# Forget-gate and stick-breaking heads walked in pairs, their value products alternating, and value products issued ahead of the transposes

## The chip, the cores and the metric

One NeuronCore of one Trainium2 chip runs the whole program. The metric is device time in microseconds (us) of one execution. A chip run of this kernel takes 1867.9 us in the median of three (1865.4 to 1868.3).

## The reference, cut to what matters

Two transformer blocks run one after the other on 512 tokens of width 1024, in fp32. The change lies in the first block, which has two layers. In a layer, after one input projection, three kinds of attention heads work side by side:

```python
# differential heads (4, value width 128): two score maps, softmax of each, w = p1 - lam * p2, then w @ v
# forget-gate heads (4, width 64):
logits = s + cqb[..., :, None] - cum_logf[..., None, :]
p = jax.nn.softmax(jnp.where(causal, logits, -jnp.inf), axis=-1)
return jnp.einsum('bhqk,bhkd->bhqd', p.astype(v.dtype), v)
# stick-breaking heads (4, width 64):
log_fail = jnp.where(strict, jax.nn.log_sigmoid(-z), 0.0)
after = lax.cumsum(log_fail, axis=3, reverse=True) - log_fail
weights = jnp.where(strict, jnp.exp(jax.nn.log_sigmoid(z) + after), 0.0)
return jnp.einsum('bhqk,bhkd->bhqd', weights.astype(v.dtype), v)
```

The head outputs are gated with silu of a projection, joined, projected with `w_out`, added to the residual and normalised. The second block has latent-attention and sparse-attention heads of width 128, a gated recurrence and a feed-forward part.

## The kernel before

**Steps.** A planner in plain Python (`plan`, L199) writes one list of steps, and each engine walks that list and issues its own share of every step. So the list is the order of work on each engine's queue, and semaphores tie the queues together.

**Items.** Attention is cut into items: one head, one tile of 128 queries, and all keys up to that tile, so tiles 0 to 3 have 1 to 4 blocks of 128 keys. Kinds are A (differential), B (forget-gate), C (stick-breaking), M (latent) and X (sparse). In a layer of the first block 16 items of kind A come first (items 0 to 15 in layer 0), then 16 of B (16 to 31) and 16 of C (32 to 47). The B and C items are laid out at L449 to L458. A unit is what shares one output bank: for A, M and X one head, for B and C two heads, of which the even one (`e=0`) writes partitions 0 to 63 of the bank and the odd one partitions 64 to 127. Before, the unit's items run e=0 tile 0 to 3, then e=1 tile 0 to 3.

**Stages and ticks.** `stages` (L240) gives each stage of an item and its lag. `tick` (L253) moves the pipeline by one item n and writes, in this order: the scores of item n, its first softmax part, the second part of n-1, the third of n-2 (kind C alone), the transposes of n-3, and the value products of n-4. What each does:

- scores (L1629, mask at L1633): TensorE, into one of two score banks. A score product must wait until the softmax of the item two before has read its bank: for kind B its logits (`soft1_done`), for kind C `soft2_done` (L1616 to L1623).
- soft1: for A, M, B and X a VectorE maximum (B: logits at L2191, maximum at L2195) and a ScalarE exponential (L1838 for B). For C three ScalarE activations, a log of one plus an exponential (L1708 to L1710).
- soft2: for B one VectorE product (L2213). For C VectorE's sum, scan and difference (L2229, L2232, L2235). soft3, C alone: ScalarE's exponential (L1855).
- trans: TensorE turns the probabilities, one transpose for each key block, into the single bank T (L1658), after the copy of the item before has emptied it. ScalarE copies T out (L1863) into one of two places PT, once the value products of the item two before are through with that place.
- pv: TensorE's value products, one for each key block (L1672), V as the stationary operand: 64 columns of it for B and C, 128 for A, M and X. They wait for that copy (L1663).

Each fp32 product shows as two matmul records in the trace.

**What lies between ticks.** `weave` (L298) places projections between ticks. A projection of 128 output columns has 24 matmuls; while items of kinds B and C are walked it is cut into two halves of 12, with a tick between and one after. For items 25 to 40 these are the gate projections. When one is whole, ScalarE and VectorE take the gate through L1708 to L1710, L2083, L1819, L2133 and L2143; in their queues that stands before the softmax of the next, even-numbered item. Weights are split by ScalarE (L1973) and GpSimd (L1435) into a high and a low part. After the last gate come splits of the gated outputs (L1989, L2456), three part projections of 18 matmuls (L1502) between ticks 40 and 44, and then `flush` (L286), which issues the remaining ticks, 44 to 51, with nothing between. The second block places its M and X ticks by hand with `paced` (L329).

## Time and profile before

| What | us |
|---|---|
| median of three runs | 1867.9 |
| the profiled execution, whole | 1866.4 |
| its span in the profile | 1864.6 |
| TensorE matmuls busy | 1730.1 (93%) |
| TensorE weight loads busy (beside the matmuls) | 1311.8 (70%) |
| VectorE busy | 864.3 (46%) |
| ScalarE busy | 799.2 (43%) |
| GpSimd busy | 594.1 (32%) |
| 16 DMA engines | 79 GB/s over the span |

The profile is one execution. Busy time is the time in which an engine had at least one instruction under way; matmuls overlap one another, so the spacing of their starts says more than their length. "PEclk" is the clock granted to TensorE as a share of the full 2.4 GHz. The mean over the span was 0.956. The first layer's items of kinds B and C run from 205 to 381 us, the second layer's from 591 to 767 us.

### The profile page before, as it was taken

The page shows a single profiled execution, that of the slowest core. Times are in us where ns is not written, and L with a number is a line of the kernel's source. Part 1 is how long each engine was busy: PE and PEld are TensorE (multiplying, and loading weights), DVE is VectorE, ACT ScalarE, POOL GpSimd, SP SyncE. Part 2 cuts the span into 40 slices and gives each one's busy share as a digit, 9 for nine tenths or more (in the row PEclk, how much of TensorE's full clock was granted, in tenths as well). Part 3 has the DMA queues.
Part 4 walks back from the last instruction along what each step waited for, and adds up shares of the span by engine and source line. Part 5 has one row for each costly group of instructions (what it writes and reads, how often), then busy time and mean ns, then how long its engine had stood idle before and what let it go on. Part 6 is the DMA issues. An engine that isn't in the chain of part 4 may idle for free. (4 is left out here: it accounts for less than half of the span.)

```text
span 1864.6 us, 21015 instructions
## 1 busy us (share of the span) xinstructions
PE 1730.1 (93%) x7750; PEld 1311.8 (70%) x7750; DVE 864.3 (46%) x1487; ACT 799.2 (43%) x1512; POOL 594.1 (32%) x291
## 2 busy tenths in 40 slices
PE   7999999889999998989998999998999899999997
PEld 4766766578667665677564777777787788888786
DVE  5543335553533345454598548475556222221402
ACT  3334446533344455344323555565643334443411
POOL 2613212135313121144120332333265424444440
PEclk9998999899989998999999999999999989999999
DMA  6412222014222120114121222322274333333221
GB/s 177 108 34 68 57 57 68 12 61 112 57 57 57 53 83 23 46 46 130 34 65 51 73 80 68 125 74 68 89 240 135 90 89 93 102 91 102 90 79 45
DMA packets 203832, 148.81 MB, mean 80 GB/s; under 512 B 14926, under 2 KB 183506, under 8 KB 203732
## 3 DMA queue, kind: packets, MB, share of 16 engines
q1 hardware_dynamic: 199056, 132.45, 24.9%
q0 software_dynamic: 4528, 14.95, 2.4%
q8 instruction: 63, 1.03, 0.2%
q14 instruction: 37, 0.30, 0.1%
q10 hardware_dynamic: 148, 0.07, 0.0%
HBM read 136.96 MB, written 10.49 MB: 79 GB/s over the span
## 5 line engine op out<-in xcount | busy, mean ns | idle before, releaser
L1435 POOL TENSOR_TENSOR weights_rounded<-weights_raw,weights_rounded 128x1024 fp32r<-128x1024 f32 (+1 forms) x237 | 566.7, 2406 | 1146.8 <-ACT weights_rounded L1973 1146.7
L1506 PE MATMUL proj<-hT_high,weights_rounded 128*128 128x512 f32 (+1 forms) x1904 | 640.2, 408 | 17.5 <-POOL weights_rounded L1435 7.5
L1506 PEld LDWEIGHTS proj<-hT_high,weights_rounded 128*128 128x128 f32 x1904 | 369.7, 195 | 108.4 <-issue 23.7
L1506 PE MATMUL proj<-hT_low,weights_rounded 128*128 128x512 f32 (+1 forms) x952 | 378.9, 398 | 0.0
L1973 ACT ACTIVATE weights_rounded<-weights_raw 128x1024 fp32r<-128x1024 f32 (+1 forms) x237 | 234.0, 1008 | 112.4 <-DMA weights_raw<-in_w_ffn_down 59.0
L1502 PE MATMUL proj<-weights_rounded,hT_high 128*128 128x512 f32 (+1 forms) x640 | 203.9, 395 | 22.2 <-DVE branches_low L2456 13.5
L1506 PEld LDWEIGHTS proj<-hT_low,weights_rounded 128*128 128x128 f32 x952 | 186.0, 195 | 38.8 <-issue 3.7
L1502 PEld LDWEIGHTS proj<-weights_rounded,hT_high 128*128 128x128 f32 x640 | 122.3, 195 | 50.9 <-issue 15.7
L1629 PE MATMUL score<-qk 64*128 64x256 f32 (+3 forms) x256 | 81.0, 501 | 18.6 <-ACT E L1835 10.2
L1672 PE MATMUL attn_out<-probs_T,V 128*64 128x128 f32 (+1 forms) x560 | 89.2, 294 | 0.0
L1658 PE MATMUL turned_probs<-constants,probs 128*128 128x128 f32 x320 | 61.8, 295 | 18.5 <-ACT probs_T L1863 18.2
L1672 PEld LDWEIGHTS attn_out<-probs_T,V 128*64 128x64 f32 (+1 forms) x560 | 68.8, 169 | 11.7 <-issue 10.0
L2175 DVE TENSOR_REDUCE small<-score 128x1 f32<-128x128 f32 (+3 forms) x64 | 28.3, 483 | 99.1 <-PE score L1633 99.1
L1502 PE MATMUL proj<-weights_rounded,hT_low 128*128 128x512 f32 (+1 forms) x192 | 72.5, 378 | 0.0
L1629 PEld LDWEIGHTS score<-qk 64*128 64x128 f32 x256 | 29.7, 190 | 54.9 <-issue 41.9
L1506 PE MATMUL score<-hT_high,weights_rounded 128*128 128x512 f32 (+2 forms) x208 | 65.4, 392 | 0.0
L1835 ACT ACTIVATE E<-score,small 128x128 f32<-128x128 f32 (+3 forms) x64 | 33.2, 524 | 68.4 <-DVE small L2175 68.4
L1708 ACT ACTIVATE tg<-proj 128x512 f32<-128x512 f32 x31 | 18.5, 597 | 101.7 <-PE proj L1506 101.7
L1754 ACT ACTIVATE qk<-proj 128x512 f32<-128x512 f32 x30 | 17.9, 597 | 92.0 <-PE proj L1506 92.0
L1863 ACT ACTIVATE probs_T<-turned_probs 128x128 f32<-128x128 f32 (+3 forms) x128 | 54.1, 423 | 5.3 <-PE turned_probs L1658 5.3
L1658 PEld LDWEIGHTS turned_probs<-constants,probs 128*128 128x128 f32 x320 | 37.8, 150 | 25.9 <-DVE probs L2213 15.1
L2083 DVE SCALAR_TENSOR_TENSOR tg<-proj,tg 128x512 f32<-128x512 f32 x20 | 13.8, 692 | 90.5 <-ACT tg L1710 90.5
(473 smaller groups left out, 2779.8 us busy)
## 6 DMA issues: line engine op xcount, KB each, us to landing
weights_raw<-in_w_in SPq DMA_DIRECT2D x113, 512.0 KB, 4.0
weights_raw<-in_w_out SPq DMA_DIRECT2D x24, 512.0 KB, 3.8
weights_raw<-in_w_ffn_gate SPq DMA_DIRECT2D x22, 512.0 KB, 3.9
weights_raw<-in_w_ffn_up SPq DMA_DIRECT2D x22, 512.0 KB, 3.8
weights_raw<-in_w_ffn_down SPq DMA_DIRECT2D x22, 512.0 KB, 3.5
gates<-constants POOLq DMA_DIRECT2D x24, 256.0 KB, 3.0
weights_raw<-gates SPq DMA_DIRECT2D x24, 256.0 KB, 3.6
weights_raw<-in_w_in SPq DMA_DIRECT2D x20, 256.0 KB, 3.2
```

Of the source, the lines that this page charges most:

```text
L1435: nc.gpsimd.tensor_tensor(piece_view(WR, p, "raw"), piece_view(WF, p, "raw"), piece_view(WR, p, "high"), ALU.subtract).then_inc(w_low, 1)
L1502: mm = nc.tensor.matmul(ps[:, 0:gr["N"]], x_[:, k, t * P:(t + 1) * P], w_[:, 0:gr["N"]], start=first, stop=last)
L1506: mm = nc.tensor.matmul(ps[:, on], w_[:, c0:c0 + P], x_[:, k, on], start=first, stop=last)
L1629: nc.tensor.matmul(ps[:, 0:K], qk[r, it["q"], tq], qk[r, it["k"], 0:K], start=True, stop=False)
L1658: mm = nc.tensor.transpose(T[:, j * P:(j + 1) * P], PR[:, i % 3, j * P:(j + 1) * P], cn("ident"))
L1672: mm = nc.tensor.matmul(O[u % 2][r0:r0 + rn, t * P:(t + 1) * P], v, PT[:, i % 2, j * P:(j + 1) * P], start=(j == 0), stop=(j == t))
L1708: link(nc.scalar.activation(dst, src, ACT.Abs, **kw))
L1754: nc.scalar.activation(plain[dst[0]](dst[1]), ps[:, :], ACT.Copy, scale=gr["scale"])\
L1835: ins = nc.scalar.activation(e[:, j, :], sc[(first_map[n] + j) % SCORE_BANKS][:, 0:K], ACT.Exp, bias=nmax[:, c + j:c + j + 1], accum_out=s ...
L1863: nc.scalar.activation(PT[:, i % 2, 0:it["K"]], T[:, 0:it["K"]], ACT.Copy).then_inc(turned_out, 1)
L1973: nc.scalar.activation(piece_view(WR, p, "high"), piece_view(WF, p, "raw"), ACT.Copy).then_inc(w_high, 1)
L2175: ins = nc.vector.tensor_reduce(nmax[:, c + j:c + j + 1], sc[(first_map[n] + j) % SCORE_BANKS][:, 0:K], AX, ALU.max, negate=True)
```

## The change

Three things are changed. The items of a B or C unit run tile by tile, e=0 and e=1 of tile 0, then both of tile 1, and so on, so that a tick's number of key blocks goes 1,1,2,2,3,3,4,4. The value products of the two items of a pair are issued together, in the tick in which the odd one is due, block by block with the two heads alternating. And in every tick, of all kinds, the value products (of n-4) are issued before the transposes (of n-3).

```diff
-    stages = [("scores", 0), ("soft1", 0), ("soft2", 1), ("soft3", 2), ("trans", 3), ("pv", 4)]
+    stages = [("scores", 0), ("soft1", 0), ("soft2", 1), ("soft3", 2), ("pv", 4), ("trans", 3)]
...
+                if name == "pv" and it["kind"] in "BC":
+                    if it["rows"][0]:
+                        steps.append(("pv", (n - lag - 1, n - lag)))
+                    continue
+                if name == "pv":
+                    steps.append(("pv", (n - lag,)))
                     continue
...
-                for e in range(2):
-                    for t in range(NT):
+                for t in range(NT):
+                    for e in range(2):
...
-                    it = items[arg]
-                    u, t, i = it["unit"], it["tile"], turned_at[arg] - 1
-                    pe.wait_ge(turned_out, i + 1)
+                    its = [items[n] for n in arg]
+                    u, t = its[0]["unit"], its[0]["tile"]
+                    pe.wait_ge(turned_out, turned_at[arg[-1]])
...
                     for j in range(t + 1):
-                        v = avv[:, j, :] if it["kind"] == "X" else V[:, j, v0:v0 + vn]
-                        mm = nc.tensor.matmul(O[u % 2][r0:r0 + rn, t * P:(t + 1) * P], v,
-                                              PT[:, i % 2, j * P:(j + 1) * P], start=(j == 0), stop=(j == t))
-                    mm.then_inc(pv_done, 1)
+                        for it, n in zip(its, arg):
+                            i = turned_at[n] - 1
+                            r0, rn = it["rows"]
+                            v0, vn = it["v"]
+                            v = avv[:, j, :] if it["kind"] == "X" else V[:, j, v0:v0 + vn]
+                            mm = nc.tensor.matmul(O[u % 2][r0:r0 + rn, t * P:(t + 1) * P], v,
+                                                  PT[:, i % 2, j * P:(j + 1) * P], start=(j == 0), stop=(j == t))
+                            if j == t:
+                                mm.then_inc(pv_done, 1)
```

No product, transpose, copy or transfer is added or taken away.

## Rows read from the trace of the kernel before

**Rows 1.** Busy us by window: length, PE, PEld, DVE, ACT, POOL, clock, DMA, GB/s.

```profile
224.00:300.00 76.00, 72.67 (x331) 49.16 (x331) 31.00 (x67) 35.55 (x76) 15.48 (x8) 0.98 0.24 70
300.00:345.00 45.00, 35.56 (x147) 24.35 (x146) 27.92 (x39) 28.93 (x59) 9.72 (x4) 0.91 0.11 36
345.00:385.00 40.00, 36.41 (x153) 23.96 (x153) 16.67 (x27) 19.41 (x43) 1.18 (x1) 0.81 0.00 0
```

**Rows 2.** TensorE's waits from 224 to 385: us in total, times, longest.

```profile
PE proj L1502 <- DVE branches_low L2456: 6.8, 3, 3.0
PE turned_probs L1658 <- ACT probs_T L1863: 5.3, 5, 1.5
PE score L1629 <- DVE logits L2235: 4.2, 3, 2.6
```

**Rows 3.** Timeline of TensorE, tick of item 23: start, length, instruction, count.

```profile
238.60 1.12 PE L1629 MATMUL score<-qk 64*128 64x512 f32 x2
...
239.72 0.28 PE L1658 MATMUL turned_probs<-constants,probs 128*128 128x128 f32 x1
239.94 1.09 PE L1672 MATMUL attn_out<-probs_T,V 128*64 128x128 f32 x8
240.95 0.50 PE L1506 MATMUL proj<-hT_high,weights_rounded 128*128 128x512 f32 x1
241.29 0.40 PE L1506 MATMUL proj<-hT_low,weights_rounded 128*128 128x512 f32 x1
```

**Rows 4.** Timeline of TensorE, a tick of a differential head.

```profile
116.86 0.70 PE L1629 MATMUL score<-qk 64*128 64x256 f32 x4
...
117.94 0.61 PE L1672 MATMUL attn_out<-probs_T,V 128*128 128x128 f32 x4
```

**Rows 5.** Timeline of TensorE, scores of items 44 and 45.

```profile
364.26 0.49 PE L1629 MATMUL score<-qk 64*128 64x128 f32 x2
...
365.43 0.70 PE L1629 MATMUL score<-qk 64*128 64x256 f32 x2
```

**Rows 6.** Timeline of TensorE, first score records of items 26 and 34 to 40.

```profile
252.66 0.59 PE L1629 MATMUL score<-qk 64*128 64x384 f32 x1
...
296.71 0.59 PE L1629 MATMUL score<-qk 64*128 64x384 f32 x1
...
302.42 1.12 PE L1629 MATMUL score<-qk 64*128 64x512 f32 x2 [0.46 <-DVE logits L2235]
...
307.72 0.37 PE L1629 MATMUL score<-qk 64*128 64x128 f32 x1
...
314.50 0.48 PE L1629 MATMUL score<-qk 64*128 64x256 f32 x1 [2.58 <-DVE logits L2235]
...
320.71 0.59 PE L1629 MATMUL score<-qk 64*128 64x384 f32 x1
...
327.14 0.69 PE L1629 MATMUL score<-qk 64*128 64x512 f32 x1 [1.18 <-DVE logits L2235]
...
332.44 0.37 PE L1629 MATMUL score<-qk 64*128 64x128 f32 x1
```

**Rows 7.** Timeline of TensorE, ticks 27 and 29; brackets: idle before, releaser.

```profile
260.07 0.30 PE L1658 MATMUL turned_probs<-constants,probs 128*128 128x128 f32 x1 [0.94 <-ACT probs_T L1863]
260.30 0.85 PEld L1672 LDWEIGHTS attn_out<-probs_T,V 128*64 128x64 f32 x8
...
270.76 0.52 PE L1658 MATMUL turned_probs<-constants,probs 128*128 128x128 f32 x3 [1.46 <-ACT probs_T L1863]
```

**Rows 8.** Timeline of VectorE, scans of stick-breaking items of 1 and 4 blocks.

```profile
366.35 0.42 DVE L2232 TENSOR_TENSOR_SCAN E<-E 128x128 f32<-128x128 f32 x1
...
374.30 1.22 DVE L2232 TENSOR_TENSOR_SCAN E<-E 128x512 f32<-128x512 f32 x1
```

**Rows 9.** Busy time after the wait at 270.76, columns as in rows 1.

```profile
271.00:275.00 4.00, 4.00 (x15) 2.98 (x14) 0.65 (x3) 1.42 (x4) 2.37 (x1) 0.59 0.03 8
```

**Rows 10.** Timeline of TensorE, value products of items 46 and 47.

```profile
378.45 2.95 PE L1672 MATMUL attn_out<-probs_T,V 128*64 128x128 f32 x14
```

More of the change, by code:

```diff
@@ L259, in tick @@
                 if (it["kind"] == "I" and lag >= 2) or (name == "soft3" and it["kind"] != "C"):
+                    continue
+                if name == "pv" and it["kind"] in "BC":
+                    if it["rows"][0]:
+                        steps.append(("pv", (n - lag - 1, n - lag)))
+                    continue
+                if name == "pv":
+                    steps.append(("pv", (n - lag,)))
                     continue
@@ L1660, in _ @@
                 elif op == "pv":
-                    it = items[arg]
-                    u, t, i = it["unit"], it["tile"], turned_at[arg] - 1
-                    pe.wait_ge(turned_out, i + 1)
+                    its = [items[n] for n in arg]
+                    u, t = its[0]["unit"], its[0]["tile"]
+                    pe.wait_ge(turned_out, turned_at[arg[-1]])
                     if u >= 2:
                         unit_done(pe, u - 2)
-                    for gg in it["values"]:
-                        wait_group(gg)
-                    r0, rn = it["rows"]
-                    v0, vn = it["v"]
+                    for it in its:
+                        for gg in it["values"]:
+                            wait_group(gg)
                     for j in range(t + 1):
-                        v = avv[:, j, :] if it["kind"] == "X" else V[:, j, v0:v0 + vn]
-                        mm = nc.tensor.matmul(O[u % 2][r0:r0 + rn, t * P:(t + 1) * P], v,
-                                              PT[:, i % 2, j * P:(j + 1) * P], start=(j == 0), stop=(j == t))
-                    mm.then_inc(pv_done, 1)
+                        for it, n in zip(its, arg):
[7 more added lines that the diff above has]
+                                mm.then_inc(pv_done, 1)
                 elif op == "down":
```

## The prediction

> **What bounds the kernel now.** I read the page's busy shares first: TensorE works 1730.1 us, 93% of the span, so time taken from it counts unless it was waiting anyway. The change touches both layers of the first block, whose two copies run alike, so I worked one out and doubled it. The busy times by stretch [rows 1] part that layer in three: forget-gate heads (72.7 of 76 us busy), then the stick-breaking heads beside the gate projections (35.6 of 45), then the last stick-breaking pair with little beside it (clock 0.81). The waits there [rows 2] say who is late: a rounded activation, ScalarE's copy of the turned probabilities, and VectorE's stick-breaking logits. The 32 items of a layer are numbered 16 to 47 below, four tiles a head, lengths of 1 to 4 key blocks ("units").
>
> **What a value product costs.** In the tick of item 23 [rows 3] eight records (four products, two records each) take 1.01 us from their start to the next projection, 0.109 each, 0.218 a unit. Around them the array changes shape. A transpose is 0.11 of stream, yet 0.22 passes before the first value record; the eight are 0.14 longer than their stream; the first projection record takes 0.34 and not 0.23. Together 0.36 us a visit to the half-width shape. A differential head, whose product is full width, shows none of that [rows 4].
>
> **Part 1, alternating halves.** The even head writes partitions 0 to 63 of the output bank, the odd one 64 to 127. No place of the trace switches between column halves. The nearest rows are the differential scores, on two halves of the array's rows: four records of 64x256 take 0.70 us, as the two of one head do [rows 4, 5]. So two halves can stream at once, here for split rows and not split columns. Bounds: a pair's unit costs from 0.218 (both at once) to 0.436 (one after the other). I take 0.218, being nearest to those rows. Its four weight loads a unit, 0.106 apart for eight in 0.85 [rows 7] when paced by the matmuls, leave an open point. The Trainium skill ("TensorE: Matmul & The Clock Gate", Packing small matmuls) reports column packing as about as good as row packing, but says in the same section that weight loads overlap running matmuls only when the row group differs. By the Trainium skill's second sentence the halves, which share all rows, would expose their loads; the trace shows loads hidden within one half [rows 7], and nothing of a switch. Rival 4 is that case.
>
> The naive sum: 80 pair units in two layers at 0.218 saved is 17.4 us, 32 fewer visits at 0.36 is 11.5 us, 28.9 us off TensorE. I don't expect it, for what follows.
>
> **Part 2, value products only in odd ticks, and tile lengths 1,1,2,2,3,3,4,4.** I went through the layer from one score product to another.
> - Items 16 to 25, until 252.66; TensorE waits for no one here. A score costs 0.21 more a unit [rows 5]. Before, score lengths sum to 10 (16-19) and 13 (20-25), after 6 and 16: -0.2 net. Value products of ticks 20-25: 13 units at 0.218 and six visits become 6 pair units at 0.218 and three visits, -2.6. Sum -2.8.
> - Items 26 to 39, start 252.66 to 332.44 [rows 6]. A gate projection ends before each even item, and then ScalarE and VectorE work through the gate (log, minimum, exponential, products) before they serve the item. For forget-gate items the next odd tick waits for the copy of the last head's turned probabilities, 7.4 us after item 26's score with 3 units in the item and 4 in the copy (252.66 to 260.07, of it idle 0.94), less with 1 and 2 units (idle 1.46) [rows 6, 7]. The value product that used to fill part of this wait moves to the odd tick. So its removal from the even tick is worth nothing. The chain stays: 7.0, 6.95 and 7.65 us with the new lengths, while TensorE is through after 4.85, 4.85 and 5.4: waits near 2.0, 1.9 and 2.0 in place of 0.94, 1.46, 0.92. Added up with the odd ticks (pair, transposes, 2.9 for the half projection), 252.66 to 296.71 becomes 42.1 against 44.05, of which 1.55 was low clock (next paragraph): -0.4 without it. For stick-breaking items the odd score waits for VectorE's logits of two items before. These cost 1.0, 1.6, 2.1 and 2.7 us at 1 to 4 units (scan 0.42 to 1.22, two others 0.29 to 0.69) [rows 8]. The waited-for lengths become 1, 2, 3 and were 2, 4, 2, so 5.2, 5.7 and 7.0 us from the even score in place of 5.7, 6.8 and 6.4. 296.71 to 332.44 becomes 31.95 against 35.73 with 1.5 of low clock: -2.25. Waits: 1.1, 1.8, 2.8.
> - The clock. After the wait of 1.46 the granted clock is 0.59 over 271 to 275, the 1.2 GHz level for most of it, which takes 1.64 us of TensorE's time, say 1.55 net; after 0.94 nothing falls [rows 7, 9]. The waits of 1.46 and 2.58 were both followed by it, two spells a layer. Now five waits are at 1.8 to 2.8; I estimate four of them with a spell, 2.2 more at 1.55: +3.4 (from -3.1, none left, to +4.7).
> - 332.44 to 345.7: ScalarE and VectorE work off gate and splits, TensorE waits up to 3.0 us for them [rows 2]; unchanged, 0.
> - 345.74 to 364.26, ticks 41 to 43. Scores 9 to 5 units, partly at the low clock, -1.3; transposes +0.3; pairs -1.2; a wait for item 38's copy, now issued later, +0.3. Sum -1.9.
> - The end, 364.26 to 381.40, where nothing lies beside it [rows 10]. Before, items 44 to 47 have 1,2,3,4 units, now 3,3,4,4. By durations in proportion to those of [rows 8] the last score goes from 6.0 to 7.4 us after the start and its probabilities are ready 14.6 and not 12.65 in. Then copy 45, pair (44,45), transposes 46, copy, transposes 47, copy and pair (46,47) follow strictly, since the pair now stands ahead of the transposes. Ends 18.5 at full clock, 21.0 at half, before 17.1. As before it runs at the half rate from 374 on, and now idles more: +2.9, between +1.4 and +3.9.
>
> **Part 3, value products ahead of transposes in single-head items.** Both wait for the same copy, so no wait is added. The turned copy is issued up to 0.87 later; a group of 24 matmuls, some 5.5 us, lies between ticks and hides it. ScalarE's queue stands behind it meanwhile, but it idles there. Only in the emptying of the sparse heads (1338 to 1344) nothing is between: +0.8, bounds 0 to +1.5. No DMA and no queue of SP or POOL is moved: the splits stand where they stood.
>
> **The sum.** A layer: -2.8 -0.4 -2.25 +3.4 -1.9 +2.9 = -1.05. Two: -2.1. With +0.8: -1.3 us on the profiled execution, whose own time is 1866.4 (span 1864.6): 1865.1. The median of the runs, 1867.9, is 1.5 above it, so I predict 1866.6.
>
> **Rivals.**
> 1. *The waits lengthen but the clock does not follow.* For: 0.94 and 1.18 us did no harm. Against: 1.46 did, and TensorE does less around them now. No more spells than two, and the end at +1.4: -2.8 -2.65 -1.9 +1.4 = -5.95 a layer, -11.1 with part 3: 1856.8.
> 2. *TensorE's saved time simply comes off*, as it would if the copies were early everywhere: -28.9, 1839. Against: the waits of [rows 2, 7].
> 3. *Slower: the two column halves don't stream at once.* Then nothing is saved by alternating, and products that filled waits are now exposed in odd ticks: 34 pair units a layer (6, 17, 7, 4 in the four stretches) at 0.218 is 7.4, and 0.9 more at the end's half clock; 16.6 for both: 1883. It decides from about a third of the overlap lost (5 us). For: no row shows split columns together. Against: the split rows. The same time comes out if the program alternates but the array keeps order.
> 4. *Weight loads stand exposed at each switch.* Four loads of 0.106 a pair unit, 34 units, twice: 29 more on top of rival 3, 1912. For: nothing in the rows. Against: within one half the loads are hidden [rows 7].
>
> **How the numbers follow.** Forecast 0.42 (1860 to 1873; 0.10 of it faster, 0.22 within, 0.10 slower), rival 1 0.26, rival 2 0.06, rival 3 0.22, rival 4 0.04. A measurement of this kernel tells about 0.2% (3.7 us) from no change. Faster 0.42, same 0.22, slower 0.36. The range reaches from below rival 1 to rival 3: 1852 to 1884, leaving out 0.06 and a little below it, and rival 4 with half the spread of rival 3 above, some 0.2 in all. The likeliest case's own range is 1860 to 1873.
>
> **What would show it.** Overlap: sixteen value records of a 4-unit pair in about 1.0 us, not 1.9. Waits: ScalarE's copy some 2 us late in three odd ticks a layer, now ahead of value products; five and not two stretches near 0.5 clock. The end of a layer at 18.5 to 21 us from item 44's score. I am wrong if gate chains shorten with TensorE's work, if spells of low clock stay at two, or if pair records come 0.109 apart.

## The result

The changed kernel takes 1872.15 us in the median of 20 runs (1867.8 to 1873.6), the kernel before 1866.9 in 20 runs beside them. The ratio is 1.0028, with a 95% interval of 1.0020 to 1.0035: slower by 0.28%, 5.2 us. I had forecast 1.3 us less than before. The range of 1852 to 1884 held the time, the sign was wrong. The profiled execution of the changed kernel took 1868.3 us (span 1866.5), so it is one of its shorter ones; its span is only 1.9 us above that of before. Six of the 20 runs took 1867.8 to 1869.4 us at a mean granted clock of 0.948 or 0.949, as this one did; the other fourteen took 1870.85 us or more, twelve of them at 0.946 or 0.947. So of the 5.2 us the traces can show about 2.

### The profile after

The head of the page, in the columns of the table of before:

```profile
span 1866.5 us, 20983 instructions
PE 1712.0 (92%) x7750; PEld 1300.9 (70%) x7750; DVE 866.6 (46%) x1487; ACT 799.6 (43%) x1512; POOL 596.2 (32%) x291
```

TensorE is busy 18.1 us less, yet the span is 1.9 us longer: all that was saved, and 2 us more, is now idle time. The three windows of [rows 1] again (length, busy time of PE, PEld, DVE, ACT, POOL, then granted clock, DMA share, GB/s):

```profile
224.00:300.00 76.00, 68.28 (x342) 47.28 (x341) 34.16 (x70) 38.57 (x84) 17.37 (x9) 0.96 0.20 63
300.00:345.00 45.00, 33.46 (x137) 22.26 (x136) 24.39 (x35) 26.34 (x52) 8.08 (x4) 0.86 0.11 36
345.00:385.00 40.00, 33.61 (x146) 21.78 (x145) 16.05 (x24) 17.73 (x38) 2.37 (x1) 0.68 0.00 0
```

Busy time fell by 4.4, 2.1 and 2.8 us, and the clock from 0.98, 0.91, 0.81 to 0.96, 0.86, 0.68. TensorE's waits in the same stretch (us in total, times, longest), against [rows 2]:

```profile
PE attn_out L1682 <- ACT probs_T L1874: 9.0, 7, 2.1
PE proj L1509 <- DVE branches_low L2467: 8.6, 3, 4.5
PE score L1636 <- DVE logits L2246: 6.3, 4, 2.7
PE turned_probs L1665 <- ACT probs_T L1874: 1.7, 2, 0.9
```

The copy of the turned probabilities is now waited for mostly by the value products and no longer by the transposes, 10.7 us in all where it was 5.3. The wait of 4.5 us ahead of the second part projection is 1.5 us longer than before, but the way from item 40's score to item 41's is not: 12.8 us against 13.3, with less of it at the low clock.

**The pair itself works as hoped.** A pair of three blocks, and two pairs of four, in TensorE's timeline (start, length, instruction, count, [idle before, releaser]):

```profile
242.84 0.88 PE L1682 MATMUL attn_out<-probs_T,V 128*64 128x128 f32 x12
...
253.96 1.76 PE L1682 MATMUL attn_out<-probs_T,V 128*64 128x128 f32 x16 [2.12 <-ACT probs_T L1874]
...
297.80 1.09 PE L1682 MATMUL attn_out<-probs_T,V 128*64 128x128 f32 x16
```

Sixteen records take 1.09 us, what eight took for one head. A pair of n blocks costs what a single head's n blocks cost (0.44, 0.66, 0.88, 1.09 us for 1 to 4). The second line has the forecast wait ahead of such a pair, and the pair is longer there, 1.76 us, as the clock falls within it (next paragraph).

**The clock.** Four short windows of the same layer, behind the waits at 253.96 (2.12 us), 266.57 (2.06), 307.56 (1.78) and 320.59 (2.72), and the two ends of the layers:

```profile
254.30:257.30 3.00, 3.00 (x19) 2.38 (x16) 0.12 (x1) 1.81 (x5) 2.37 (x1) 0.50 0.00 0
268.00:271.00 3.00, 3.00 (x9) 2.32 (x8) 0.00 (x0) 0.34 (x2) 1.92 (x1) 0.50 0.03 8
309.00:312.00 3.00, 3.00 (x10) 2.43 (x9) 0.55 (x1) 1.84 (x5) 2.13 (x1) 0.50 0.00 0
322.60:325.60 3.00, 3.00 (x10) 2.42 (x9) 2.07 (x2) 2.05 (x4) 0.30 (x1) 0.50 0.00 0
...
360.00:384.00 24.00, 18.73 (x73) 11.25 (x72) 11.16 (x15) 11.86 (x22) 2.37 (x1) 0.50 0.00 1
749.00:773.00 24.00, 18.75 (x71) 11.48 (x72) 10.46 (x14) 11.19 (x21) 2.38 (x1) 0.50 0.00 1
```

A clock of 0.50 is the 1.2 GHz level for the whole window. All four spells are short. The last two lines are the new thing: 24 us on end at half rate where the layer ends, in both layers (the clock record has 23.9 us, from 360.0 and from 749.2). Before, the spell there was 6.8 us long (from 374.1).

**The end of the layer.** From item 44's score to the output projection:

```profile
356.33 0.91 PE L1636 MATMUL score<-qk 64*128 64x384 f32 x2
...
359.64 0.44 PE L1682 MATMUL attn_out<-probs_T,V 128*64 128x128 f32 x4 [1.12 <-ACT probs_T L1874]
360.01 0.69 PE L1665 MATMUL turned_probs<-constants,probs 128*128 128x128 f32 x2
361.35 2.07 PE L1636 MATMUL score<-qk 64*128 64x512 f32 x2 [0.65 <-DVE logits L2246]
...
369.25 0.87 PE L1665 MATMUL turned_probs<-constants,probs 128*128 128x128 f32 x3 [0.90 <-ACT probs_T L1874]
370.70 1.55 PE L1682 MATMUL attn_out<-probs_T,V 128*64 128x128 f32 x12 [0.58 <-ACT probs_T L1874]
372.18 1.12 PE L1665 MATMUL turned_probs<-constants,probs 128*128 128x128 f32 x4
374.07 1.09 PE L1665 MATMUL turned_probs<-constants,probs 128*128 128x128 f32 x4 [0.78 <-ACT probs_T L1874]
375.85 1.97 PE L1682 MATMUL attn_out<-probs_T,V 128*64 128x128 f32 x16 [0.69 <-ACT probs_T L1874]
379.39 0.77 PE L1509 MATMUL proj<-weights_rounded,hT_high 128*128 128x512 f32 x1 [1.57 <-DVE branches_low L2467]
```

The drain, from item 44's score to the end of the last value product, is 21.5 us; before it was 17.1 [rows 5, 10]. The projection behind it starts at half rate: 0.77 us for its first record. Its first 114 matmuls take 28.2 us from 379.39, before 26.1.

Stretches from score to score in the two traces, in us, layer 0 | layer 1 (from the first score record of the item named; the end of the drain is that of the last value product):

| Stretch | before | after | difference | forecast |
|---|---|---|---|---|
| items 16 to 26 | 47.7, 47.7 | 45.0, 45.0 | -2.7, -2.7 | -2.8 |
| items 26 to 40 | 79.8, 79.7 | 80.2, 78.6 | +0.5, -1.1 | +0.75 (-0.4 -2.25 +3.4) |
| items 40 to 44 | 31.8, 31.8 | 29.1, 30.3 | -2.7, -1.5 | -1.9 |
| drain | 17.1, 17.1 | 21.5, 21.5 | +4.4, +4.4 | +2.9 |
| first 114 matmuls of the projection | 26.1, 26.1 | 28.2, 28.6 | +2.1, +2.5 | 0 |
| from there to the next layer or block | 58.2, 84.4 | 59.3, 82.7 | +1.1, -1.7 | 0 |

Part of these differences is the low clock's place. Over items 40 to 44 it covers 13.6 us before in both layers, and after 6.8 us in layer 0 and 13.6 in layer 1. So layer 1's -1.5 is the one to hold against the forecast of -1.9. Over items 26 to 40 two spells became four in layer 0 and three in layer 1.

### The profile page after: what moved, and what is told of

Read it like the earlier page. It is cut to its first block and busy times, and to the rows that moved or that the text cites. A ratio compares the mean times of both kernels' runs of the same rounds, so it can differ in the third digit from the quotient of the medians.

```text
span 1866.5 us, 20983 instructions
## 1 busy us (share of the span) xinstructions
PE 1712.0 (92%) x7750; PEld 1300.9 (70%) x7750; DVE 866.6 (46%) x1487; ACT 799.6 (43%) x1512; POOL 596.2 (32%) x291
## 5 line engine op out<-in xcount | busy, mean ns | idle before, releaser
L1984 ACT ACTIVATE weights_rounded<-weights_raw 128x1024 fp32r<-128x1024 f32 (+1 forms) x237 | 233.9, 1008 | 116.8 <-DMA weights_raw<-in_w_ffn_down 58.2
L1509 PEld LDWEIGHTS proj<-weights_rounded,hT_high 128*128 128x128 f32 x640 | 124.8, 199 | 52.4 <-issue 15.6
L1636 PE MATMUL score<-qk 64*128 64x128 f32 (+3 forms) x256 | 83.1, 506 | 22.8 <-DVE logits L2246 12.8
L1682 PE MATMUL attn_out<-probs_T,V 128*64 128x128 f32 (+1 forms) x560 | 68.0, 314 | 19.8 <-ACT probs_T L1874 19.6
L2186 DVE TENSOR_REDUCE small<-score 128x1 f32<-128x128 f32 (+3 forms) x64 | 28.3, 483 | 96.2 <-PE score L1640 96.2
L1636 PEld LDWEIGHTS score<-qk 64*128 64x128 f32 x256 | 30.3, 192 | 59.6 <-issue 40.8
L1682 PEld LDWEIGHTS attn_out<-probs_T,V 128*64 128x64 f32 (+1 forms) x560 | 52.4, 177 | 25.7 <-ACT probs_T L1874 23.8
L1509 PE MATMUL proj<-weights_rounded,branches_low 128*128 128x512 f32 x128 | 53.1, 415 | 0.0
```

Source lines behind the costliest of these rows:

```text
L1509: mm = nc.tensor.matmul(ps[:, 0:gr["N"]], x_[:, k, t * P:(t + 1) * P], w_[:, 0:gr["N"]], start=first, stop=last)
L1636: nc.tensor.matmul(ps[:, 0:K], qk[r, it["q"], tq], qk[r, it["k"], 0:K], start=True, stop=False)
L1682: mm = nc.tensor.matmul(O[u % 2][r0:r0 + rn, t * P:(t + 1) * P], v, PT[:, i % 2, j * P:(j + 1) * P], start=(j == 0), stop=(j == t))
L1984: nc.scalar.activation(piece_view(WR, p, "high"), piece_view(WF, p, "raw"), ACT.Copy).then_inc(w_high, 1)
L2186: ins = nc.vector.tensor_reduce(nmax[:, c + j:c + j + 1], sc[(first_map[n] + j) % SCORE_BANKS][:, 0:K], AX, ALU.max, negate=True)
```

## The experiments

All were timed beside the kernel before. A ratio is against it, with its 95% interval. 0.001 of it is 1.9 us. Diffs are against the kernel named.

### Does the alternation make the overlap?

`in_turn`: the change, with the pair's second head issued behind the first.

```diff
-                    for j in range(t + 1):
-                        for it, n in zip(its, arg):
+                    for it, n in zip(its, arg):
+                        for j in range(t + 1):
```

> The changed kernel, but the two heads of a pair have their value products one head after the other, not alternating. Theory (the overlap of the two column halves is had in full, and what is lost is lost at the end of each layer): a pair unit costs 0.436 and not 0.218 us wherever TensorE is what is late, 34 pair units a layer and 0.9 at the low clock: 8.3 us a layer, 1872.2 + 16.6 = 1889. Rival (TensorE reorders the records across the halves by itself, as it does across row halves in the differential scores, or the pair's time is hidden by waits): 1872 to 1874.

Measured: 1874.1 us, ratio 1.0047 (1.0035 to 1.0059), where the rival had it. By the ratios that is only some 3.5 us above the change, and the two intervals meet at 1.0035. The lines of its pairs of two, three and four blocks (the last at full clock):

```profile
237.11 0.67 PE L1682 MATMUL attn_out<-probs_T,V 128*64 128x128 f32 x8
...
245.17 1.15 PE L1682 MATMUL attn_out<-probs_T,V 128*64 128x128 f32 x12
...
301.12 1.58 PE L1682 MATMUL attn_out<-probs_T,V 128*64 128x128 f32 x16
```

With two blocks the pair is as short as the alternating one (0.66); with three it takes 1.15 us, not 0.88, with four 1.58, not 1.09. Even then it is shorter than eight blocks in a row would be. In the two-block pair the eight records start two by two (237.114 and 237.127, 237.275 and 237.287, ...). All eight fit in the time of four, which they can't if the second head's records wait for the first head's last. In the three-block pair the second head's first record starts at 245.445, and the first head's last one, which carries its signal, at 245.767. In all 32 pairs of this trace the second head's records begin when four of the first head's are left, or at once where it has no more than four. So the other half's matmuls run ahead of the program's order, by up to four records. Whether TensorE's queue or the step that compiles the program makes this order is not shown. The Trainium skill ("TensorE: Matmul & The Clock Gate", Part 3, What overlaps and what doesn't) says that matmuls start and end in program order, with no reordering, and that a weight load overlaps only when the row group differs. By that this kernel would have shown the single head's spacing and the change the exposed loads of rival 4. The trace shows neither. Alternation in the program is worth little, because most of the overlap comes without it.

### Which part of the change loses?

`tiles_only`: the kernel before, with the tile order alone.

```diff
-                for e in range(2):
-                    for t in range(NT):
+                for t in range(NT):
+                    for e in range(2):
```

> The kernel before with one part of the change: the items of a unit run tile by tile (lengths 1,1,2,2,3,3,4,4); value products stay single, in every tick, behind the transposes. Theory (the end of a layer loses because its last items are long): the end from item 44's score on takes some 19 us and not 17.1, the low clock reaches into the output projection, stretches before it gain 2 to 3 us a layer: 1868 to 1873 in all. Rival (the waits beside the gate projections are what costs): those come from value products leaving the even ticks, which is not done here, so 1867 or below.

`order_only`: the kernel before, with value products ahead of the transposes alone.

```diff
-    stages = [("scores", 0), ("soft1", 0), ("soft2", 1), ("soft3", 2), ("trans", 3), ("pv", 4)]
+    stages = [("scores", 0), ("soft1", 0), ("soft2", 1), ("soft3", 2), ("pv", 4), ("trans", 3)]
```

> The kernel before with one part of the change: value products ahead of the transposes in every tick, single, items in the old order. Theory: nothing moves where a projection lies between ticks. In the empty end of a layer the copy, the value products and the next transposes stand in a row, 1 to 1.5 us a layer, and under 0.8 at the end of the sparse heads: 1868 to 1870. Rival (the order itself is the loss): 1871 or above.

Measured: `tiles_only` 1864.1 us, ratio 0.9997 (0.9986 to 1.0008); `order_only` 1862.2, ratio 0.9983 (0.9973 to 0.9992). Neither part alone is slower. `tiles_only` is where its rival had it, and both miss their theories (1868 to 1873, 1868 to 1870). In the trace of `tiles_only` the drain is 20.4 and 21.7 us, so the longer drain is the tile order's; what the rest of the layer gives (124.2 us from item 16 to 40, before 127.5) pays for most of it. The projection behind it takes 26.1 us in both layers, as before. `order_only` has a drain of 18.8 us and a projection of 28.1 in layer 0, but 16.2 and 26.1 in layer 1. The loss is where the parts meet.

### Is it the end of the layer?

`all_but_last`: the change, with the last unit of each layer as before (head by head, no pairs, value products behind the transposes). The single value products of the other kinds stand behind the transposes too.

```diff
-    stages = [("scores", 0), ("soft1", 0), ("soft2", 1), ("soft3", 2), ("pv", 4), ("trans", 3)]
+    stages = [("scores", 0), ("soft1", 0), ("soft2", 1), ("soft3", 2), ("pair", 4), ("trans", 3), ("single", 4)]
...
+                if name in ("pair", "single"):
+                    if it["kind"] == "I" or (name == "pair") != it.get("pair", False):
+                        continue
+                    if name == "single":
+                        steps.append(("pv", (n - lag,)))
...
-                for t in range(NT):
-                    for e in range(2):
-                        its.append(dict(kind=kind, head=2 * c + e, tile=t, K=P * (t + 1), maps=1,
+                for e, t in ([(e, t) for e in range(2) for t in range(NT)] if kind + str(c) == "C1" else [(e, t) for t in range(NT) for e in range(2)]):
+                    if True:
+                        its.append(dict(kind=kind, pair=(kind + str(c) != "C1"), head=2 * c + e, tile=t, K=P * (t + 1), maps=1,
```

> The changed kernel, but the last unit of each layer (stick-breaking heads 2 and 3, items 40 to 47) runs as before: head after head, single value products behind the transposes, and so do all items outside the pairs. Theory (the end is what loses): the gains of the stretches up to item 40 stay, 2.3 to 4 us a layer, the end is that of before: 1859 to 1863. Rival (the waits beside the gate projections are what costs, they are all still there): 1869 or above.

Measured: 1852.0 us, ratio 0.9928 (0.9916 to 0.9940), further down than any theory said. The window of the drain and that of the projection:

```profile
361.00:380.00 19.00, 14.71 (x73) 9.67 (x72) 8.75 (x15) 11.99 (x28) 0.00 (x0) 0.82 0.00 1
380.00:406.00 26.00, 26.00 (x115) 21.42 (x116) 12.79 (x17) 5.33 (x9) 6.29 (x3) 1.00 0.24 82
```

The drains are short again, 17.4 and 15.6 us, and the projection runs at full clock from its first matmul, 26.1 us. The profiled execution took 1856.7 us, the longest of the five, so its trace shows 9.7 of the 13.4 us.

`last_unit_alone` is the converse: the kernel before, with the last unit of each layer alone as in the change. It has the stages of `all_but_last`, and

```diff
+                for e, t in ([(e, t) for t in range(NT) for e in range(2)] if kind + str(c) == "C1" else [(e, t) for e in range(2) for t in range(NT)]):
+                    if True:
+                        its.append(dict(kind=kind, pair=(kind + str(c) == "C1"), head=2 * c + e, tile=t, K=P * (t + 1), maps=1,
```

> The kernel before, with the last unit of each layer alone as in the change: tile by tile rising, in pairs, ahead of the transposes; the three other units and all other heads in the old order. Theory (the end of the layer is where the change loses, by some 5 to 7 us a layer, and the other units gain about as much): the loss stands alone, 1873 to 1881. Rival (the last unit loses only because the units before it have got shorter, and the clock or the pending work then falls out badly): 1864 to 1869.

Measured: 1876.7 us, ratio 1.0050 (1.0032 to 1.0068). The unit loses by itself, some 9 us by the ratio (6 to 13), with the same signs: drains of 21.5 us in both layers, the first 114 projection matmuls 28.4. Four of its six runs took 1876.7 to 1877.7 us at a mean clock of 0.947 to 0.949, the other two 1868.4 and 1869.4 at 0.956. The rival, that it loses only because the units before it got shorter, falls; that it loses more because of them does not (see the table below).

### What in the last unit?

Three kernels stand between `all_but_last` and the change. `last_single` walks the last unit tile by tile without pairs, `last_behind` pairs it but behind the transposes, `others_behind` puts the pair ahead of them.

The first is, against `all_but_last`:

```diff
-                for e, t in ([(e, t) for e in range(2) for t in range(NT)] if kind + str(c) == "C1" else [(e, t) for t in range(NT) for e in range(2)]):
+                for e, t in [(e, t) for t in range(NT) for e in range(2)]:
```

`others_behind` has, besides, `pair=True` for every unit. `last_behind` is that with these lines in place of the stages and of the test that sorts pairs from single items:

```diff
+    stages = [("scores", 0), ("soft1", 0), ("soft2", 1), ("soft3", 2), ("pair", 4), ("trans", 3), ("late", 4), ("single", 4)]
...
+                    last = it["kind"] == "C" and it["head"] > 1
+                    if it["kind"] == "I" or name != ("late" if last else "pair" if it.get("pair") else "single"):
+                        continue
```

> As the change, but the last unit of a layer, though it walks its two heads tile by tile, gives each item's value products in a step of its own, without pairs, behind the transposes, as do the other heads. It differs from the kernel with the last unit wholly in the old order (1852) by the tile order of that unit alone. Theory A (tile order): 1862 to 1868. Theory B (place and pairing): 1851 to 1856.

> Pairs and rising tiles in all units as in the change; in the last unit of a layer the pair's value products stand behind the transposes of the step, and so do the single value products of the other heads everywhere. Theory A (of the end's loss it is the tile order that makes it, the longest items last): about as the change, 1866 to 1871. Theory B (it is the place of the value products: in the last steps nothing but the transposes can fill the time that they give): the end falls back by 3 to 4 us a layer, 1858 to 1863.

> The change with one edit: the single value products of the differential, sparse and max-score heads stand behind the transposes, as in the kernel before; pairs and rising tiles as in the change. Theory (the change loses at the end of each layer and nowhere else): 1869 to 1873, as the change, whose stretches outside the forget-gate and stick-breaking units moved by under 1 us in all. Rival (those single value products cost the change a part of its 5 us): 1863 to 1868. It is also the base from which the kernels with another last unit were cut.

Measured: 1860.5 (0.9967, 0.9954 to 0.9979), 1866.45 (1.0006, 0.9997 to 1.0016) and 1868.1 us (1.0019, 1.0010 to 1.0027). Neither of the two theories holds alone. `last_single` was to be 1862 to 1868 by the tile order or 1851 to 1856 by place and pairing and falls between. `last_behind` sits at the lower edge of the tile order's range, and `others_behind` between its theory and its rival: the place of the pair is worth about 2 us, not 3 to 4 a layer. The windows of drain and projection, first `last_single`, then `last_behind`:

```profile
356.70:379.20 22.50, 18.10 (x72) 10.20 (x71) 10.65 (x15) 13.35 (x28) 0.00 (x0) 0.70 0.00 1
379.20:405.40 26.20, 26.12 (x116) 21.59 (x117) 12.93 (x17) 5.55 (x9) 6.37 (x3) 1.00 0.24 81
```

```profile
355.00:378.00 23.00, 16.37 (x72) 8.54 (x71) 10.54 (x14) 13.23 (x28) 0.00 (x0) 0.60 0.00 1
378.00:407.00 29.00, 28.79 (x117) 23.59 (x118) 13.12 (x19) 5.79 (x10) 6.46 (x3) 0.90 0.21 73
```

The drains differ by 0.6 us, yet the pairs leave TensorE 1.7 us less busy in it (16.37 against 18.10), the low clock lasts to 383.6 and not to 375.1, and the projection takes 28.7 and not 26.1 us. That is 3.2 us a layer in the traces, 6.3 of the 7.3 that the ratios say. The overlap of the halves saves matmul time where nothing can use it, and TensorE comes to the projection at half rate.

The trace of `in_turn`, whose pairs overlap in part only, bears this out. Its windows of drain and projection in layer 0:

```profile
359.40:382.30 22.90, 18.30 (x72) 10.09 (x71) 9.24 (x13) 12.04 (x26) 0.00 (x0) 0.57 0.00 1
383.80:410.00 26.20, 26.20 (x117) 21.62 (x118) 12.88 (x18) 5.53 (x9) 6.44 (x3) 1.00 0.23 81
```

TensorE is busy longer, the low clock ends 0.9 us before the projection starts, and that takes 26.1 us in both layers. Drain and projection together take 49.0 and 47.3 us, in the change 49.7 and 50.1: the ends of the layers are shorter with the longer matmuls. `in_turn` is slower all the same by what it loses elsewhere, most in items 26 to 40 of layer 1 (84.2 us, in the change 78.6).

`three_rising_unpaired` splits the gain of the three other units: the kernel before with those three tile by tile, unpaired. In place of the two loops it has

```diff
+                for e, t in ([(e, t) for e in range(2) for t in range(NT)] if kind + str(c) == "C1" else [(e, t) for t in range(NT) for e in range(2)]):
```

> The kernel before, with three of the four forget-gate and stick-breaking units of a layer walked tile by tile, rising, without pairs; the last one in the old order. It tells what of the 14 us that the change gains in these three units is the tile order's and what the pairs'. Theory A (the order's: two heads' long items stand together, where before one head's drain stood under the other's short items): 1852 to 1857. Theory B (the pairs': 16 value products in the time of 8): 1862 to 1866, level with before.

Measured: 1862.5 us, 0.9984 (0.9975 to 0.9993). Theory B: the pairs make most of it. With that the change can be taken apart in steps, each the difference of two ratios, in us of 1866 (each uncertain by about 2 to 3):

| Step | kernel reached | ratio | us |
|---|---|---|---|
| three units tile by tile | `three_rising_unpaired` | 0.9984 | -3.0 |
| those in pairs, ahead of the transposes | `all_but_last` | 0.9928 | -10.4 |
| last unit tile by tile | `last_single` | 0.9967 | +7.3 |
| last unit in pairs, behind | `last_behind` | 1.0006 | +7.3 |
| that pair ahead of the transposes | `others_behind` | 1.0019 | +2.4 |
| the other kinds' value products ahead | the change | 1.0028 | +1.7 |

The intervals on either side of each of the last two steps overlap, so these two are not shown each by itself.

The steps hold in this order only. The three steps in the last unit cost 17 us on top of three paired units; on the kernel before, the same edits to the last unit cost 9 (`last_unit_alone`). Its tile order costs 7.3 us here, but 2.4 where the other three units are unpaired (`tiles_only` at 0.9997 against `three_rising_unpaired` at 0.9984). So the last unit loses by itself, and loses more once the units before it are paired. Why it does is not shown.

### Is it the rising order?

`last_descending`: pairs everywhere, the last unit's tiles falling (3, 3, 2, 2, 1, 1, 0, 0), the others rising. `all_descending`: all units falling. Both are cut from `others_behind`, with the other kinds' value products behind the transposes. `change_falling`: the change with this one edit.

```diff
-                for t in range(NT):
+                for t in reversed(range(NT)):
```

> Pairs in all forget-gate and stick-breaking units, ahead of the transposes, as in the change; only the last unit of a layer walks its tiles from the longest to the shortest (3, 3, 2, 2, 1, 1, 0, 0), and the single value products of the sparse, differential and max-score heads stand behind the transposes again. Theory (what the change loses, it loses at the end of the layer, where its two longest items come last and nothing is left to stand beside them): the drain behind the last score covers 128-column items, some 10 us instead of 21.5, so that the end gains some 6 us a layer on the change and 2 on the kernel before: 1848 to 1858, at or below the kernel that leaves the last unit in the old order (1852). Rival A (it is the value products standing ahead of the transposes that loses at the end, whatever the lengths): 1862 to 1868. Rival B (beginning the last unit with its longest tiles puts two 512-column scans behind two others and makes TensorE wait there for what the end gives back): 1860 to 1866.

> As the change, but every forget-gate and stick-breaking unit walks its tiles from the longest to the shortest, and the single value products of the other heads stand behind the transposes. Theory (a unit loses where its long pair is followed by work that can't cover it): each unit ends on 128-column items and hands over to the next one's longest, whose scans of 1.2 us come on VectorE together; the ends of the layers gain 6 us each, the middles lose 1 to 4 us a layer by waits for the first long items: 1850 to 1864. Rival (the waits of the rising order between two units, 2 us and more before items 24 to 26, are what the order costs, and a falling order has none): 1842 to 1850.

> The change with one edit: each forget-gate and stick-breaking unit walks its tiles from the longest to the shortest; all value products, the other heads' too, stay ahead of the transposes. It differs from the kernel with all units falling and the other heads' value products behind (1847.9) in that last point alone. Theory (the change loses by the rising order, which puts its longest pairs last): 1846 to 1854. Rival (the other heads' value products ahead of the transposes, among them those of the differential heads that stand before the forget-gate ones, cost a share of the 5 us): 1854 to 1860.

Measured: 1858.05 (0.9954, 0.9941 to 0.9967), 1847.85 (0.9903, 0.9890 to 0.9917) and 1853.5 us (0.9936, 0.9922 to 0.9950). The first and the last lie at the upper edge of what the theory said, the second in the range of its rival. The drain is 12.6 us in `last_descending` and 12.5 to 13.4 in the others, a little above the 10 that I had written. One line turns the change from 5.2 us slower into 12 us faster than the kernel before. `last_descending`, where its two longest items follow two longest ones of the unit before, gives part back: from item 40 to 44 it takes 30.9 and 34.2 us, and `all_descending` 26.1. The difference between `all_descending` and `change_falling`, 6 us by the ratios, comes with the other kinds' value products ahead of the transposes: more than the 1.7 above. How they cost it is not shown. In the traces 6.2 us of it lies in items 26 to 40 of layer 0 (83.0 us against 76.8), where the low clock covers 17.1 us and 3.4; yet layer 1 of `all_descending`, with those products behind, takes 83.0 us for the same stretch. Another 2.1 lies behind the last sparse item's score (534.2 against 532.1 us to the end of the span), and `last_descending`, with them behind, has 534.0.

`falling_alone`: the kernel before with every unit tile by tile and falling; no pairs, value products behind the transposes. `last_unit_falling`: the same for the last unit alone. `falling_last_unpaired`: all units falling, pairs in all but the last.

```diff
 falling_alone (against the kernel before):
-                for e in range(2):
-                    for t in range(NT):
+                for t in reversed(range(NT)):
+                    for e in range(2):
 last_unit_falling (against the kernel before):
+                for e, t in ([(e, t) for t in reversed(range(NT)) for e in range(2)] if kind + str(c) == "C1" else [(e, t) for e in range(2) for t in range(NT)]):
 falling_last_unpaired (against all_descending):
-                        its.append(dict(kind=kind, pair=True, head=2 * c + e, tile=t, K=P * (t + 1), maps=1,
+                        its.append(dict(kind=kind, pair=(kind + str(c) != "C1"), head=2 * c + e, tile=t, K=P * (t + 1), maps=1,
```

> The kernel before with one edit: forget-gate and stick-breaking units are walked tile by tile over their two heads, from the longest tile to the shortest; no pairs, and value products behind the transposes as before. Theory A (the gain of the falling order with pairs, 19 us on the kernel before, is made by the order alone: each unit's drain gets short and the long items' scans meet a full queue): 1846 to 1854. Theory B (it needs the pairs, whose 16 value products take the time of 8 ahead of the transposes): the order gives the two ends, 2 to 4 us each, and the rest is the pairs': 1857 to 1864. Rising and tile by tile without pairs was 1864, level with before.

> The kernel before, with the last unit of each layer alone walked tile by tile from the longest to the shortest, without pairs. Theory (the end of a layer is set by what stands behind its last score): the drain is 12 instead of 17 us and the low clock there 7 to 10 instead of 20 us, so 5 to 8 us a layer less, with 1 to 3 back where the unit begins with two 512-column items: 1854 to 1860. Rival (the gain of the falling order is in the units before): 1863 to 1867.

> All forget-gate and stick-breaking units falling (3, 3, 2, 2, 1, 1, 0, 0); pairs ahead of the transposes in all but the last unit of a layer, whose items give their value products one by one behind the transposes, as the other heads do. Theory (pairs pay within a layer and cost at its end, by the low clock that reaches some 4 us into the output projection, 28.2 instead of 26.1 us for its first 114 matmuls): the middles of the kernel with pairs everywhere (1847.9) and the end of the one without any (1849.5), 1840 to 1846. Rival (the two gains are one and the same, TensorE waits for the score chain either way): 1846 to 1851.

Measured: `falling_alone` 1849.5 us, 0.9918 (0.9905 to 0.9931): theory A, the order without any pair is worth most of it. `last_unit_falling` 1862.9 us, 0.9983 (0.9975 to 0.9992): above what the theory said. Its drain is 12.0 us as expected, but from item 40 to 44 it takes 34.2 us (before 31.8). The longer of two spells of low clock there lasts 13.7 us, before 10.2, and comes again for 3.4 us as the projection starts:

```profile
344.00:358.00 14.00, 12.64 (x33) 7.44 (x34) 8.50 (x10) 5.29 (x10) 0.76 (x1) 0.51 0.00 0
367.40:379.50 12.10, 11.24 (x69) 7.35 (x68) 5.13 (x13) 8.54 (x26) 0.00 (x0) 1.00 0.00 1
381.00:408.70 27.70, 27.70 (x116) 22.65 (x117) 12.81 (x17) 5.42 (x9) 6.33 (x3) 0.94 0.22 77
```

So a short drain alone is worth 3 us, for both layers; the rest of the falling order's gain of 15 needs the units before it to fall too.

`falling_last_unpaired` takes 1843.0 us, 0.9879 (0.9862 to 0.9896), the fastest of all, 1.2% under the kernel before. Its end, from the drain on:

```profile
358.00:371.00 13.00, 11.34 (x69) 7.35 (x68) 5.92 (x14) 9.25 (x27) 0.00 (x0) 1.00 0.01 1
372.00:398.00 26.00, 26.00 (x118) 21.45 (x117) 12.68 (x18) 5.32 (x9) 6.56 (x3) 1.00 0.24 82
```

The drain is 12.0 us at full clock, and the projection takes 26.1. Pairs pay within a layer: 7 us against `falling_alone`, with intervals that lie apart. That they cost at its end the times alone don't show, since the intervals of this kernel and of `all_descending` (0.9890 to 0.9917) overlap from 0.9890 to 0.9896. The traces do: with the last unit paired the drain takes 13.4 and 13.3 us in the two layers and not 12.0, and the projection 28.2 and 28.3 and not 26.1.

## Why the prediction was wrong

**Overlap of the halves (part 1): right.** 0.218 us a pair unit was taken, 16 records in 1.09 us came. Rivals 3 and 4 fall, and with them the 0.26 that they had. (Rival 3 counts 4 pair units in the last stretch, whose pairs have 1, 2, 3 and 4 blocks, 10 in all, and gives no reason for leaving out six.) The alternating order, which I had taken for its cause, is worth some 3.5 us by `in_turn`.

**The stretches up to item 44: right in the waits, and a little better than forecast.** Sum forecast -3.95, measured -5.0 and -5.3; 1.2 us of layer 0's -2.7 over items 40 to 44 is luck, a shorter spell of low clock, as layer 1 shows with -1.5. The waits ahead of the odd ticks came as worked out: 2.12, 2.06, 2.01 us (forecast 2.0, 1.9, 2.0) before value products and 1.13, 1.78, 2.72 (1.1, 1.8, 2.8) before stick-breaking scores. Five waits between 1.8 and 2.8, four of them with a low clock behind in layer 0, as said, and three in layer 1: rival 1 falls too. (Four spells for two would be +3.1; the +3.4 of the sum takes 2.2 more.)

**The end: the step that failed.** The prediction has it "at the half rate from 374 on" and takes +2.9 with bounds of +1.4 and +3.9. The trace has the half rate from 360 on for 23.9 us. I let the added waits lengthen the drain by their own time, and kept the clock as it was. The chain of copies and products itself was right: at half rate throughout the prediction had the end 21.0 us in, and it came at 21.5. But these are the waits of 1.12, 0.65, 0.90, 0.58, 0.78 and 0.69 us in one row, with overlapped pairs between them, and behind them the clock stays down. It cost twice: the drain takes +4.4, above my bound, and the output projection starts 4.5 and 5.4 us before the clock is back, +2.1 and +2.5. The second term was not in the sum at all; I had ended the layer at its last value product. Together +6.5 and +6.9 where +2.9 stood: 3.6 and 4.0 us a layer, 7.6 for both. The change of the median was missed by 6.5 us. That 1872.15 lies in the likeliest case's range is luck in part: with each bounded term at its slow end (+4.7, +3.9, +1.5) the sum gives 1871.9, and it has no term for the projection. The experiments bear the step out: with the last unit as before the change gains 13 us, with the last unit alone changed it loses 9, and the four kernels whose last unit rises in alternating pairs have a projection of 28.2 to 28.8 us, the two that rise without pairs (`tiles_only`, `last_single`) 26.1. The drains of those two are 20.4 to 21.7 us, so most of the first cost comes with the rising order and the second with the pairs.

**The sparse heads' emptying (part 3): right in itself.** From the last sparse item's score to the next projection 11.5 us became 12.2, +0.65 against +0.8. But from that score to the end of the span it is 534.3 us against 531.9 before, with 2.3 us more of low clock in it. Those value products are not shown to be the cause: `order_only` has them ahead too and takes 532.1, `last_descending` has them behind and takes 534.0, and the other kernels with them behind lie between 531.3 and 532.2. A term for this was not in the sum.

**What lies beyond.** The traces also differ where nothing was changed, by where the low clock falls: a spell of 6.8 us at 97.7 before is absent after, and item 16 starts 3.0 us earlier. Such terms go both ways and cancel in part. From the traces I get +1.9, from the medians +5.2; where the other executions of the changed kernel lose the rest is open. Their mean granted clock is lower (0.946 against 0.949), which does not say where.

**The naive sum** (28.9 us off TensorE) is not lost everywhere: 10 us of it come in the three units that have projections beside them, and in the last unit, with nothing beside its drain, pairs cost 7.

## What to carry to other kernels

Cheaper matmuls gain where other TensorE work waits behind them. In the drain here the same saving turned into idle time, and the next stage paid for it at the low clock, so carry the sum one stage beyond the end. Order the items of a pipeline so that the last ones to be drained are the shortest, and let the units before it fall in the same way, so that one unit's long items don't follow another's. Apply pairing unit by unit: here the best kernel pairs three units of four.

## What the runs showed of the hardware

Matmuls on the two column halves of the array run side by side with fp32 operands: 16 records in 1.09 us where one half's 8 take 1.09. Their weight loads stay hidden although both use all rows. They overlap even when the program gives one half's products behind the other's: wholly with two blocks each (0.67 us), in part with three and four (1.15 and 1.58 us, against 0.88 and 1.09 alternating). In all 32 pairs of `in_turn` the second half's records start when no more than four of the first half's are left.

The length of a drain doesn't tell how long the low clock lasts. Drains of 21.0 and 21.6 us (`last_single`, `last_behind`) had it end 4.2 us ahead of the projection in one kernel and 5.4 us into it in the other, with TensorE busy 18.1 and 16.4 us of their windows. The drains of 12.0 us, three kernels and both layers, ran at full clock throughout.
